# A hybrid decoder layer on one core: selection work for ScalarE, convolution taps for VectorE, page numbers loaded once, norm waits by halves

## What is computed

```python
h = x + 0.5 * g1 * swiglu(modulate(x, g_ffn1, s1, sc1), w1_gate, w1_up, w1_down)
n = modulate(h, g_mix, s2, sc2)                 # rmsnorm(h) * (1 + scale) + shift
z = n @ w_in        # conv GLU | q | k | v | indexer q, k, head weights | two branch gates
conv: GLU -> causal depthwise convolution, 31 taps, 512 channels -> LayerNorm -> silu -> w_conv_out
attention: score[t,s] = sum_h w[t,h] * relu(qi[t,h] . ki[s]); keep the top 256 (prompt)
           or 65 (samples) admissible keys; softmax attention over them -> w_attn_o
h = h + g2 * ((sigmoid(g_c) * conv + sigmoid(g_a) * att) @ w_out)
h = h + 0.5 * g3 * swiglu(modulate(h, g_ffn2, s3, sc3), w2_gate, w2_up, w2_down)
y = rmsnorm(h, g_final)
```

## Time and profile before

| | |
|---|---|
| median of 3 runs | 2641.59 us (2638.42 to 2644.48) |
| the profiled execution | 2641.7 us, of which the span in the profile 2639.9 |
| mean granted TensorE clock | 0.97 of full speed |
| TensorE, VectorE, ScalarE, GpSimd busy | 94%, 53%, 25%, 55% |
| first logits of the prompt (L2144) | at 1535.08 us |

### The profile page before, as it was taken

The page is one execution under the profiler, slowest core; times in us unless marked ns, Lnnn a source line. Parts: engine busy times, 40 slices in busy tenths (PEclk is TensorE's granted clock), DMA queues, the critical chain, the costliest instruction groups (busy, mean ns, idle before and its releaser), DMA issues.

```text
span 2639.9 us, 44639 instructions
## 1 busy us (share of the span) xinstructions
PE 2485.7 (94%) x16038; PEld 2307.2 (87%) x16038; DVE 1401.2 (53%) x2619; ACT 662.7 (25%) x1238; POOL 1458.6 (55%) x1234
## 2 busy tenths in 40 slices
PE   5999999999998888899999779999899999999997
PEld 3899999999997756699998446789799999999997
DVE  5543334434446638799998445462564444444444
ACT  3311011111112323335544457310511111111113
POOL 1276666666665325536999020124057777777774
PEclk8999999999999879999999969999999999999999
DMA  8422222222221532231224600334011111111112
GB/s 288 120 68 77 72 67 68 79 79 79 73 79 53 151 74 77 75 102 49 79 92 145 220 11 1 98 98 146 1 33 48 49 53 50 53 49 48 48 48 82
DMA packets 243128, 209.99 MB, mean 80 GB/s; under 512 B 14687, under 2 KB 207315, under 8 KB 241993
## 3 DMA queue, kind: packets, MB, share of 16 engines
q1 hardware_dynamic: 232844, 181.70, 22.9%
q10 hardware_dynamic: 10181, 26.90, 3.2%
HBM read 173.03 MB, written 28.94 MB: 77 GB/s over the span
## 4 chain that ended last, share of the span: by engine, by line
PE 82%; DVE 6%; issue 4%; SPq 3%; ACT 3%; POOL 1%; DMA 0%; ACTq 0%; DVEq 0%; POOLq 0%
PE main L763 11%; PE main L764 10%; PE main L765 10%; PE main L295 7%; PE main L296 7%; PE main L297 7%; PE main L864 5%; PE main L865 5%; PE main L866 5%; SPq L1925 2%; DVE pick L1742 2%; PE main L2144 2%; PE main L2161 1%; PE aux L2172 1%; PE aux L763 1%
## 5 line engine op out<-in xcount | busy, mean ns | idle before, releaser
L684 POOL TENSOR_TENSOR blo<-raw,bhi 128x512 fp32r<-128x512 f32 x424 | 553.5, 1306 | 34.0
L682 POOL CAST bhi<-raw 128x512 fp32r<-128x512 f32 x424 | 264.7, 624 | 544.8 <-PE main L866 311.4
L763 PE MATMUL main<-nhi,bhi 128*128 128x352 f32 x1312 | 429.1, 327 | 17.9 <-issue 10.8
L764 PE MATMUL main<-nlo,bhi 128*128 128x352 f32 x1312 | 423.0, 322 | 0.0
L765 PE MATMUL main<-nhi,blo 128*128 128x352 f32 x1312 | 422.8, 322 | 0.0
L295 PE MATMUL main<-nhi,whi 128*128 128x352 f32 x1032 | 340.3, 330 | 1.0 <-DVE pick_s L1730 0.5
L297 PE MATMUL main<-nhi,wlo 128*128 128x352 f32 x1032 | 334.1, 324 | 0.0
L296 PE MATMUL main<-nlo,whi 128*128 128x352 f32 x1032 | 334.1, 324 | 0.0
L1100 DVE SCALAR_TENSOR_TENSOR h<-main,ada,h 128x352 f32<-128x352 f32 (+1 forms) x448 | 251.9, 570 | 84.5 <-PE main L866 84.5
L864 PE MATMUL main<-hid_hi,bhi 128*128 128x352 f32 x896 | 292.1, 326 | 4.7 <-DVE h L1100 2.8
L282 POOL CAST whi<-raw 128x1024 fp32r<-128x1024 f32 x51 | 56.4, 1106 | 422.0 <-issue 234.6
(11 more groups left out here) (379 smaller groups left out, 5130.7 us busy)
## 6 DMA issues: line engine op xcount, KB each, us to landing
raw<-in_w_gate SPq DMA_DIRECT2D x44, 512.0 KB, 4.1
raw<-in_w_up SPq DMA_DIRECT2D x44, 512.0 KB, 3.9
ada_part<-in_w_ada SPq DMA_DIRECT2D x44, 512.0 KB, 5.0
raw<-in_w_down SPq DMA_DIRECT2D x44, 512.0 KB, 3.9
raw<-in_w_in SPq DMA_DIRECT2D x40, 512.0 KB, 3.9
ada_raw<-in_w_ada SPq DMA_DIRECT2D x7, 2048.0 KB, 12.0
gate_d<-zraw ACTq DMA_DIRECT2D x16, 528.0 KB, 2.7
gates<-gate_d SPq DMA_DIRECT2D x16, 528.0 KB, 4.7
```

The costliest lines, as they stand in the source:

```text
L682: pool.tensor_copy(bhi[:, slot], src).then_inc(sg.block_hi.sem, 1)
L684: pool.tensor_tensor(blo[:, slot], src, bhi[:, slot].bitcast(F32), ALU.subtract)\
L763: pe.matmul(out, bhi[:, slot, w], hi(c), start=start and c == 0, stop=False, skip_group_check=True)
L764: pe.matmul(out, bhi[:, slot, w], lo(c), start=False, stop=False, skip_group_check=True)
```

## The change

* Selection: `SIGN_BLOCKS` becomes (0, 5), so ScalarE also counts the narrowest block (384 wide), and its counts stand every 1.18 evacuations instead of 1.3.
* Convolution: `LEFT` goes from 4 to 16. Twelve of group 1's taps go from ScalarE's products and GpSimd's additions to VectorE. `PRODUCTS_AT` gives two products for each of tiles 21 to 36 and three for each of the last four (before: two for tiles 21 to 24, three for all after).
* Page numbers: SyncE loads the 16 page numbers one by one in its loop over the last 16 tiles of the input projection, each behind that tile's DMA, and keeps them in registers (`page_of`). The key and value pages use these.
* Norm waits: `ready` takes a half. TensorE waits for the half that it is about to use: per unit in `pe_first` of both FFNs, and in `m1_pe` for tile 0 ahead of its first chunk and again in the middle.

```diff
--- before.py
+++ after.py
@@ -535,8 +535,8 @@
                 dve.tensor_tensor(nlo[:, c4s[half], tcs(t)], tmp[:, c4s[half], :],
                                   nhi[:, c4s[half], tcs(t)].bitcast(F32), ALU.subtract).then_inc(s["lo"], 1)
 
-            def ready(pe, t):
-                norm_wait(pe, q, "lo", 2 * t + 2)
+            def ready(pe, t, half=1):
+                norm_wait(pe, q, "lo", 2 * t + half + 1)
             return {"gather": gather, "total": total, "square_act": square_act, "square_more": square_more, "square_pool": square_pool, "square_dve": square_dve,
                     "root": root, "inverse": inverse,
                     "scale": scale, "affine": affine, "low": low, "ready": ready}
@@ -774,9 +774,9 @@
                 pe.wait_ge(*banks_free)
                 for t in range(NTC):
                     for m in range(2):
-                        if m == 0:
-                            nrm["ready"](pe, t)
                         for half in range(2):
+                            if m == 0:
+                                nrm["ready"](pe, t, half)
                             sg.block_ready.wait(pe, 2 * m + half + 1)
                             pe_unit(pe, 2 * m + half, X(half, t), bank(3 * m + t), half == 0, half == 1)
                         nrm["pe_between"](pe, 2 * t + m)
@@ -1171,7 +1171,7 @@
         equal = aux[:, :, :].rearrange("p a n -> p (a n)")
         rank = place("rank", [P, SEQ], F32, UB + 29696)
         over, miss, sgn, taken = (place(n, [P, 6], F32) for n in ("over", "miss", "sgn", "taken"))
-        SIGN_BLOCKS = (0,)
+        SIGN_BLOCKS = (0, 5)
         NSIGN = len(SIGN_BLOCKS)
         odd = place("odd", [P, NSIGN, SEQ], F32, HB + 2 * 4 * TOK)
         signs = place("signs", [P, 2, SEQ], BF16, UB + 29696)
@@ -1238,6 +1238,8 @@
             n = 2 * (6 * (L - Z_Q - 1) + 2 * t + half)
             return range(n, n + 2) if L > Z_Q and n < len(PIECES) else range(0)
 
+        page_of = []
+
         def m1_sp(sp):
             for L in range(3):
                 first.block_ready.wait(sp, NBLOCKS - (4, 2, 0)[L])
@@ -1269,6 +1271,10 @@
                          allow_slow_non_contiguous=True).then_inc(wr_in, 16)
             for L in range(Z_Q + 1, NZ):
                 load_tile(sp, T_Z + L, L % RING, cols(w_in, ZCOL[L]))
+                n = L - (NZ - 2 * NSEQ)
+                if n >= 0:
+                    page_of.append(sp.value_load(a["page_table"][n // 2:n // 2 + 1, n % 2:n % 2 + 1], min_val=0,
+                                                 max_val=L0["cache_k"].shape[0] - 1))
 
         def m1_pool(pool):
             def post(L):
@@ -1346,8 +1352,9 @@
         def m1_pe(pe):
             for t in range(NTC):
                 for L in range(2):
-                    norm_m["ready"](pe, t)
-                    z_product(pe, L, T_Z + L, L % RING, 3 * L, L % 2, 72 if L == 0 else P, ts=(t,))
+                    norm_m["ready"](pe, t, L)
+                    z_product(pe, L, T_Z + L, L % RING, 3 * L, L % 2, 72 if L == 0 else P, ts=(t,),
+                              middle=(lambda t: norm_m["ready"](pe, t)) if L == 0 else None)
                     if (L, t) == (0, 0):
                         norm_m["total"](pe, 2)
             for L in range(2, Z_Q):
@@ -1428,7 +1435,7 @@
 
         def sign_counts_at(L, t):
             e = 3 * (L - Z_V - 1) + t
-            return [n for n in range(SIGN_BIT - 1) if int(2.0 + 1.3 * n) == e]
+            return [n for n in range(SIGN_BIT - 1) if int(2.0 + 1.18 * n) == e]
 
         def evac(act, dst, L, func, then):
 
@@ -1778,7 +1785,7 @@
                     .then_inc(cv, 1)
 
         CV_DEC = 4 * 2 + 1
-        LEFT = 4
+        LEFT = 16
         CV_TOTAL = CV_DEC + 2 * CW + LEFT
 
         def conv_group(dve, c):
@@ -1799,7 +1806,7 @@
         NPROD = 2 * (CW - 1) - LEFT
         PRODUCTS_AT, made = {}, 0
         for L in range(Z_GLU + 4, NZ):
-            n = 2 if L < Z_GATE else 3
+            n = 2 if L < NZ - 4 else 3
             PRODUCTS_AT[L] = list(range(made, made + n))
             made += n
         assert made == NPROD
@@ -1922,9 +1929,7 @@
                 load_tile(sp, T_MIX + m, (T_MIX + m) % RING, mix_load(m))
             def pages(b, cache, dst, done):
                 for pg in range(2):
-                    page = sp.value_load(a["page_table"][b:b + 1, pg:pg + 1], min_val=0,
-                                         max_val=cache.shape[0] - 1)
-                    sp.dma_start(dst[:, pg, :], cache[bass.ds(page, 1)].rearrange("o p h d -> (o p) (h d)"))\
+                    sp.dma_start(dst[:, pg, :], cache[bass.ds(page_of[2 * b + pg], 1)].rearrange("o p h d -> (o p) (h d)"))\
                         .then_inc(done, 16)
 
             def keys_of(b):
```

## The result

The kernel after takes 2627.74 us (median of 12 executions, 2622.32 to 2633.80), the kernel before 2642.34 us (12 executions, 2638.16 to 2652.51). The ratio is 0.9945 with a 95% interval of 0.9931 to 0.9960. The forecast was 2623.5 us, with a range of 2615 to 2632. The profiled execution took 2624.34 us with a span of 2622.5 us; its twin of before took 2641.7 us, so the two profiles differ by 17.4 us where the sum said 18.2.

The account below looks back on a forecast made before the run. TensorE, busy 94% of the span, was taken as the bound, so only its waits or lower clock pay. Gains of 13.1 + 3.4 + 1.7 = 18.2 us from 2641.7 gave 2623.5 us, range 2615 to 2632.

Parts of the forecast that it names:

- Part 1: Sample attention: page numbers in registers remove TensorE's 12.2 us value-page wait; first logits 13.1 us earlier.
- Parts 2 and 3: Selection and convolution: ScalarE's second block saves VectorE 15 us, twelve more taps cost 15.7; effect on the time 0.
- Part 4: Norm waits by halves: gain 3.4 us in the first FFN, 1.7 in the mixer, 0 in the second FFN.
- halves give nothing: Rival at both norm chains: another link holds them, only the 13.1 us remain, 2628.6 us; chance 0.06.
- The contention rival: Before the LayerNorm: value pages slow key-token stores, costing about 4 us, at worst 8.4; 2627.5 us; chance 0.12.
- The clock rival: Logits' first 28 us: TensorE at the upper clock once the long gap is gone, 6 us more; 2617.5 us; chance 0.14.
- The other two rivals: Page numbers loaded again at use, 2636.6 us, chance 0.04; ScalarE and VectorE taking turns in selection, 2671, chance 0.04.

Follow-up runs that it names:

- pages_only: Kernel before with only the page numbers kept in registers, loaded in SyncE's input loop; 2629.36 us, ratio 0.9937.
- whole3: Kernel after with the second FFN alone waiting for whole norms (both halves) again; 2627.99 us, ratio 0.9920.
- halves_only: Kernel before with only the norm waits by halves; 2643.09 us, ratio 0.9992.
- after_again: Kernel after, unchanged, run a second time; 2625.55 us, ratio 0.9932.
- mask_first: Kernel after with VectorE's mask of the second value half ahead of the second LayerNorm scaling's multiplication; 2630.86 us, ratio 0.9951.
- pool_late: Kernel after with GpSimd's split of the second FFN's sixth weight block waiting for VectorE's second x sum; 2623.98 us, ratio 0.9906.
- select_only: Kernel before with only the second selection block on ScalarE, closer slots and twelve more taps on VectorE; 2645.35 us, ratio 0.9999.
- left29: Kernel after with the second selection block back on VectorE, slots at 1.3, and 29 taps instead of 16 on VectorE; 2628.84 us, ratio 0.9937.
- late_ka: Kernel after with the load of all keys moved behind the last key pages and that of the queries behind the value pages; 2629.24 us, ratio 0.9950.

## Why the prediction was right, and where two steps failed

**Part 1** (13.1 us forecast) measured 13.05 in the profile after and 12.9 in pages_only. The chain named as late next, the second LayerNorm scaling ahead of the mask, is the one found. That the figure is met to 0.1 us is in part luck: the kernel after repeated has 14.2, mainly since its LayerNorm sums ran at the upper level for longer. The loads of the page numbers hid as costed: SyncE's waits for the splits fell from 471.3 to 431.7 us, by nearly the 43 us that the loads may take.

**Parts 2 and 3** (0 forecast) measured 0 (ratio 0.9999 to within 0.0015). VectorE's rounds take 4.45 us, forecast 4.5:

```profile
1140.18 0.22 DVE L1630 TENSOR_SCALAR bound_s<-aux 128x1 f32<-128x1 f32 x2
...
1144.63 0.23 DVE L1630 TENSOR_SCALAR bound_s<-aux 128x1 f32<-128x1 f32 x2
```

(the bounds at the start of two successive rounds). The convolution ends at 1463.1. **The taps were mis-sized, the smaller of the two steps that failed:** 1.81 us each in the kernel after (28.97 us for sixteen) where the step had 1.31; the 20 us of cover swallowed it. Ten of them took 1.28 us; the six that ran beside GpSimd's splits of the mixing weights (to 1450.1) took 1.94 or 3.25. A first row has these six, a second the kernel before, where taps that add into PSUM (`aux`) and not into SBUF (`conv_y`) ran beside the same splits:

```profile
L1784 DVE SCALAR_TENSOR_TENSOR conv_y<-uext,taps,conv_y 128x1024 f32<-128x1024 f32 x6 | 15.6, 2598 | 0.2
```

```profile
L1793 DVE SCALAR_TENSOR_TENSOR aux<-uext,taps,aux 128x1024 f32<-128x1024 f32 x8 | 10.3, 1289 | 1.4 <-DVE aux L1793 1.4
```

The split's subtraction takes 3.2 us beside the first and 2.36 beside the second. So this is the collision of the second FFN once more, and it depends on where VectorE's operands lie. The price of 1.31 came from four taps that had no split beside them.

**Part 4.** First FFN: 3.4 forecast. TensorE's idle time before it fell from 10.84 to 7.34 us and its start moved by 4.1. Mixer: 1.7 forecast, 1.7 measured (5.83 us ahead at the last third's first matmul, of which 4.10 were there before). The wait itself became 4.8 us and not 3.9, because TensorE no longer waited 0.7 us for the third before and came to this one sooner. Second FFN: forecast 0, with a gain of up to 1.9 as the other end. Measured: +3.5 us, a loss. **This is the step that failed and cost time.** It said that VectorE's chain from the last low part "is its own" and that TensorE meets it again at 1923.78. It does, but the chain is not its own: its sums take turns with GpSimd's splits, and the earlier units start those earlier. whole3, halves_only and pages_only agree on it. With this loss the halves as a whole give nothing that can be told (0.9992), which is the outcome of the rival "halves give nothing" (2628.6), though not by its reason: both norm chains moved.

**The contention rival** (0.12) was given as another outcome, but something like a mild form of it may have come with the forecast: ahead of the LayerNorm, in the value tokens rather than the key tokens, whose stores landed in 2.0 us where the earlier trace rows has 2.8. The longest issue of a value-token store took 1.6 to 2.3 us in the profiles of the kernel after, after_again, whole3, pages_only, mask_first and pool_late, and 0.4 to 1.0 in the three without the page numbers (the kernel before, halves_only and select_only), but also only 0.55 in left29, which has them. The stage's +1.8 us is not all of this making, since halves_only has +1.1 as well. The median, 2627.7, lies on this rival's 2627.5, which is chance: its own stage lost 1.8 us, the second FFN 3.5, and the input products won 2.9. What late_ka and left29 show is how near the large form was.

**The clock rival** (0.14) fell: 0.50 granted in the logits' first 28 us, as before. Here a rule of the Trainium skill, "TensorE: Matmul & The Clock Gate", "What's actually happening", was weighed: the gate closes after idling and opens with activity. The trace had 2.6 and 0.7 us of idling ahead of the logits and the clock was down; by that rule in the form the prediction gave it, it would have stayed up.

**The other two rivals** fell: the pages took 0.91 us each, so nothing was loaded again, and with rounds of 4.45 us the engines did not take turns. (That rival took SyncE's mean wait, 12.4 us, for a tile's period; evacuations come 3.8 us apart, so it is 11.4.)

**Not forecast:** 2.9 us in the input products. The same kernel has +1.1 there in after_again, so this is scatter between executions rather than the change. Nearly all of it arises between 945 and 1130 us, beside the indexer scores, where the clock falls to 0.50 for short stretches: three of them behind 970 us in the kernel after, four in the kernel before, five in after_again, one of these twice as long as the others.

By its own profile the sum reads -4.1 (-3.4), -1.7 (-1.7), -13.05 (-13.1), +3.5 (0), +1.8 (0) and -3.8 (0) for the rest: two losses that were missed, 5.3 us, and 3.8 us the other way, mostly scatter. That the total of the profiles was only 0.8 us off is in part luck. The median lies 3.4 us above the profiled execution; losses in the first 60 us, as in the seven profiles above, would do that, but those executions have no profile.

## What to carry to other kernels

A wait that is made finer doesn't only let its own engine start earlier. It gives buffers back earlier, and the engine that refills them may then run beside the one on the critical path: cost the refill too, and look at the duration of the critical instructions where they would overlap. Where loads are made quicker to issue, ask what else is on the DMA engines in that stretch, and issue the ones with slack behind the stores that somebody waits for. Price an instruction beside the neighbours that it will have: the same tap took 1.28 us alone and up to 3.25 beside GpSimd. A pause of TensorE can cost more than its length, since the lower level behind it took another 1.5 to 2.0 us here. And where single executions scatter by more than a step is worth, compare the same matmul in both traces, stage by stage.

## What the runs showed of the hardware

VectorE's tensor_tensor of 128x1408 with both operands in SBUF took 1.62 us alone and up to 2.71 us beside GpSimd's cast or subtraction; those took up to 2.0 and 2.55 us instead of 0.61 and 1.29, each side waiting out the other's instruction. A convolution tap of 128x1024 took 1.28 us alone, 1.94 or 3.25 beside GpSimd's splits when it added into SBUF, and 1.29 beside such splits when it added into PSUM. This was in no term of the sum.

ScalarE's issue of one 256 KB store took 2.15 us where its neighbours took 0.34 to 0.37, in a stretch with 344 GB/s moving; what makes it stall is open, since with 393 GB/s beside the same stores in left29 none took over 0.55. And in 16 us near the start (36 to 52 us) the same code was granted 1.00 in one execution and 0.50 in another; profiles that met this lost up to 9.9 us.
